# Output products bank by bank with resident weight tiles, and row norms by token tile: a two-block network on one Trainium2 core

## What is computed

```python
def rmsnorm(x, w):
    xf = x.astype(jnp.float32)
    y = xf * lax.rsqrt(jnp.mean(xf * xf, axis=-1, keepdims=True) + EPS)
    return (y * w.astype(jnp.float32)).astype(x.dtype)
...
        xn = rmsnorm(h, mix_norm_w[l])
        proj = xn @ w_in[l]
...
        merged = jax.nn.sigmoid(gate_a) * y_a + jax.nn.sigmoid(gate_b) * y_b
        h = h + merged @ w_mix_out[l]
        h = h + peer_ffn(rmsnorm(h, ffn_norm_w[l]), peer_w_query[l], peer_keys_1[l],
                         peer_keys_2[l], peer_down[l], peer_up[l])
    return rmsnorm(h, final_norm_w)
...
    merged = g_ssd * y_ssd + g_sb * y_sb
    out = jnp.einsum('bld,de->ble', merged, w_out)
    return x + rmsnorm_2(out, norm_post)
```

## Time and profile before

| | us |
|---|---|
| median of three runs | 3337.38 |
| lowest and highest | 3335.16, 3338.36 |
| the profiled execution | 3326.07 |
| its span, first to last instruction | 3324.4 |
| TensorE matmul busy in it | 3052.6 |
| VectorE, ScalarE, POOL busy | 1907.9, 1157.4, 482.5 |

### The profile page before, as it was taken

The page is one execution under the profiler, slowest core; times in us unless marked ns, Lnnn a source line. Parts: engine busy times, 40 slices in busy tenths (PEclk is TensorE's granted clock), DMA queues, the critical chain, the costliest instruction groups (busy, mean ns, idle before and its releaser), DMA issues. The chain is left out here.

```text
span 3324.4 us, 43992 instructions
## 1 busy us (share of the span) xinstructions
PE 3052.6 (92%) x14376; PEld 2458.6 (74%) x14376; DVE 1907.9 (57%) x3582; ACT 1157.4 (35%) x1735; POOL 482.5 (15%) x672
## 2 busy tenths in 40 slices
PE   6999999969897869999999999999996999989996
PEld 4688877757676657788888888888884767866885
DVE  4574444338888968655555565555554674445332
ACT  4443342222236752223323222222233332355222
POOL 1023350000247950000000000000000031024000
PEclk9999999979899989999999999999998989989998
DMA  2220003322223444343333343343332211200331
GB/s 100 76 64 21 26 23 114 103 68 70 70 76 123 180 179 141 123 126 121 118 112 116 126 126 120 120 125 115 126 101 77 86 41 57 89 13 6 122 96 63
DMA packets 136432, 312.39 MB, mean 94 GB/s; under 512 B 9104, under 2 KB 74768, under 8 KB 134160
## 3 DMA queue, kind: packets, MB, share of 16 engines
q1 hardware_dynamic: 136160, 311.00, 28.5%
q10 hardware_dynamic: 176, 0.11, 0.0%
HBM read 273.33 MB, written 37.75 MB: 94 GB/s over the span
## 5 line engine op out<-in xcount | busy, mean ns | idle before, releaser
L180 ACT ACTIVATE split<-raw 128x1024 fp32r<-128x1024 f32 x440 | 455.1, 1054 | 1227.0 <-PE up L1303 457.9
L189 DVE TENSOR_TENSOR split<-raw,split 128x1024 fp32r<-128x1024 f32 x408 | 491.7, 1224 | 551.8 <-ACT split L180 542.1
L1301 PE MATMUL up<-split,weight_high 128*128 128x512 f32 x1024 | 400.4, 391 | 19.6 <-DVE weight_low L1855 19.6
L1302 PE MATMUL up<-split,weight_high 128*128 128x512 f32 x1024 | 399.2, 390 | 0.0
L1303 PE MATMUL up<-split,weight_low 128*128 128x512 f32 x1024 | 399.0, 390 | 0.0
L2001 DVE TENSOR_TENSOR h<-h,up 128x512 f32<-128x512 f32 x416 | 269.3, 683 | 108.1 <-PE up L1303 108.1
L1937 PE MATMUL down<-xh,split 128*128 128x512 f32 x832 | 323.8, 389 | 1.8 <-ACTq L1958 1.8
L1938 PE MATMUL down<-xl,split 128*128 128x512 f32 x832 | 323.7, 389 | 0.0
L1939 PE MATMUL down<-xh,split 128*128 128x512 f32 x832 | 323.6, 389 | 0.0
L1301 PEld LDWEIGHTS up<-split,weight_high 128*128 128x128 f32 x1024 | 192.6, 188 | 63.7 <-issue 19.8
L2306 POOL TENSOR_TENSOR dec<-dec,upto 128x512 f32<-128x512 f32 x16 | 20.0, 1274 | 1483.0 <-ACT dec L2297 1483.0
(11 more groups left out here) (443 smaller groups left out, 5882.5 us busy)
## 6 DMA issues: line engine op xcount, KB each, us to landing
raw<-in_stream SPq DMA_DIRECT2D x440, 512.0 KB, 3.5
gates<-stage SPq DMA_DIRECT2D x16, 2048.0 KB, 6.5
gate<-gates SPq DMA_DIRECT2D x32, 1024.0 KB, 7.4
h<-in_x SPq DMA_DIRECT2D x2, 2048.0 KB, 7.8
rows<-h SPq DMA_DIRECT2D x1, 2048.0 KB, 6.6
h<-rows SPq DMA_DIRECT2D x1, 2048.0 KB, 7.9
out<-res SPq DMA_DIRECT2D x4, 512.0 KB, 2.8
keys<-in_keys SPq DMA_DIRECT2D x1, 1024.0 KB, 4.9
```

Of the source, the lines that this page charges most:

```text
L180: act.activation(g.high[t % slots], g.raw[:, t % RAW, :], ACT.Copy).then_inc(g.high_split, 1)
L189: dve.tensor_tensor(g.low[t % slots], g.raw[:, t % RAW, :], g.high[t % slots], ALU.subtract).then_inc(g.low_split, 1)
L1301: pe.matmul(bank, xh, hi[:, w], start=start, stop=False, skip_group_check=True)
L1302: pe.matmul(bank, xh, lo[:, w], start=False, stop=False, skip_group_check=True)
```

## The change

**Norms by token tile.** A class `TokenNorm` does the norm for one token tile at a time: square, root, scaling, then transposes of its eight 128 x 128 pieces into two banks, and two column steps, each on four chunks at once (128 x 4 x 128). The weight of the norm is now an operand that is broadcast along the tokens, in a tensor_tensor. `opening` replaces `setup` and the first `normed_columns`: one block, h in four transfers, the columns, `ws` and the heads' constants on ScalarE's queue, the two stream splits inside, `ident` made first on POOL. On VectorE each tile's root and scaling stand ahead of the tile before's column steps; a column step waits until the narrow product has used its buffer, and TensorE transposes a tile only behind the narrow products of the one before (`narrow`: eight fp32 products of 128 columns a tile). The second block's `normed_columns` stays.

**Output products bank by bank.** The loops are swapped: bank 0 goes through all eight tiles, then bank 1, and so on. The six tiles beyond the two slots have their own places in SBUF (`out_tile`). `mix_out_norm` is the first block's stage: three PSUM banks in turn for the products, the add behind each bank, the ffn norm of token tile t while later banks are multiplied, and the keys loaded behind the stream. `mix_out_finish` is the last stage: eight banks, and square, root, product, add and store by token tile (stores by half token tile). The old `mix_out`, `finish` and `setup` go.

The diff, cut to its core (the removed functions are in the listing above; what `TokenNorm`'s methods compute is what `normed_columns` computed):

```diff
+    def turn(self, pe, t):
+        pe.wait_ge(self.scaled, t + 1)
+        banks = len(self.turned_ps)
+        for half in range(2):
+            k = 2 * t + half
+            if k >= banks:
+                pe.wait_ge(self.columned, k - banks + 1)
+            for c in range(TT):
+                at = (TT * half + c) * P
+                last = pe.transpose(self.turned_ps[k % banks][:, c * P:c * P + P], self.rows[:, t % 2, at:at + P],
+                                    self.g.ident[:, :])
+            last.then_inc(self.turned, 1)
...
+    def columns(self, dve, t, weight):
+        g = self.g
...
+                if self.small:
+                    dve.wait_ge(self.small_used, k - 1)
+            w = COLS[weight][0] + TT * half
+            dve.tensor_tensor(self.col[:, k % 2, :, :],
+                              self.turned_ps[k % len(self.turned_ps)][:, :].rearrange("p (c n) -> p c n", n=P),
+                              g.cols[:, w:w + TT].unsqueeze(2).to_broadcast([P, TT, P]),
+                              ALU.mult).then_inc(self.columned, 1)
...
+def opening(g, weight, small):
...
+            @block.sync
+            def _(sp):
+                for t in range(TT):
+                    sp.dma_start(g.h[:, t, :], io["x"][t * P:t * P + P, :]).then_inc(rows_loaded[t], 16)
+                for j in range(RAW):
+                    sp.dma_start(g.raw[:, j, :], io["stream"][place(j)]).then_inc(g.raw_loaded[j], 16)
...
+                act.sem_inc(g.tile_used, 2)
+                for t in range(TT):
+                    act.wait_ge(rows_loaded[t], 16)
+                    norm.square(act, t)
+                    norm.root_scalar(act, t)
+                    if t:
+                        norm.split_columns(act, t - 1)
+                    if t >= 2:
+                        split_high(g, act, 0, t - 2)
...
+                pe.wait_ge(ident_made, 2)
+                for t in range(TT):
+                    norm.turn(pe, t)
+                    norm.narrow(pe, t)
...
+def out_bank(g, pe, slots, q, bank, done):
+    w = slice(q // 2 * P, q // 2 * P + P)
+    for c in range(N_OUT):
+        if q == 0:
+            pe.wait_ge(g.low_split, g.base + c + 1)
+        last = mm_rows(pe, slots.high[c], slots.low[c], bank[:, :], g.mh[:, c, w], g.ml[:, c, w], q % 2, c == 0,
+                       c == N_OUT - 1)
+        if q == 2 * TT - 1 and c < N_OUT - 1:
+            last.then_inc(g.tile_used, 1)
+    last.then_inc(done, 1)
+    if q == 2 * TT - 1:
+        pe.wait_ge(done, 2 * TT)
+        pe.sem_inc(g.tile_used, 1)
+def mix_out_norm(g, weight, keys_page):
...
+            @block.sync
+            def _(sp):
+                stream_load_each(g, sp, N_OUT)
+                sp.dma_start(g.keys[:, :, :], g.io["keys"]).then_inc(keys_loaded, 16)
+                sp.wait_ge(keys_loaded, 16)
+            @block.tensor
+            def _(pe):
                 for q in range(2 * TT):
...
+                    if q >= 3:
+                        pe.wait_ge(added, q - 2)
+                    out_bank(g, pe, slots, q, out[q % 3], done)
+                    if q % 2 and q >= 3:
+                        norm.turn(pe, q // 2 - 1)
+                norm.turn(pe, TT - 1)
...
+                for t in range(TT):
+                    act.wait_ge(added, 2 * t + 2)
+                    norm.square(act, t)
+                    norm.root_scalar(act, t)
+                    if t:
+                        norm.split_columns(act, t - 1)
+                for c in range(2):
+                    split_high(g, act, 0, N_OUT + c)
+                norm.split_columns(act, TT - 1)
...
+                for c in range(2, N_OUT):
+                    out_split_low(g, dve, slots, c)
+                for t in range(TT):
+                    for q in (2 * t, 2 * t + 1):
+                        dve.wait_ge(done, q + 1)
+                        rows = g.h[:, t, q % 2 * 512:q % 2 * 512 + 512]
+                        dve.tensor_tensor(rows, rows, out[q % 3][:, :], ALU.add).then_inc(added, 1)
+                    norm.root_vector(dve, t)
+                    norm.scale(dve, t)
+                    if t:
+                        norm.columns(dve, t - 1, weight)
+                norm.columns(dve, TT - 1, weight)
...
+def mix_out_finish(g):
...
+            @block.sync
+            def _(sp):
+                sp.dma_start(wp[:, :], g.io["norm_post"]).then_inc(loaded, 16)
+                stream_load_each(g, sp, N_OUT)
                 for q in range(2 * TT):
...
+                    rows, w = slice(q // 2 * P, q // 2 * P + P), slice(q % 2 * 512, q % 2 * 512 + 512)
+                    sp.wait_ge(added, q + 1)
+                    sp.dma_start(g.io["out"][rows, w], res[:, q // 2, w]).then_inc(stored, 16)
+                sp.wait_ge(stored, 16 * 2 * TT)
...
+            @block.scalar
+            def _(act):
+                for c in range(2, N_OUT):
+                    out_split_high(g, act, slots, c)
+                for t in range(TT):
+                    for q in (2 * t, 2 * t + 1):
+                        act.wait_ge(done, q + 1)
+                        if q:
+                            act.wait_ge(summed, q)
+                        act.activation(junk[:, :], out[q][:, :], ACT.Square,
+                                       accum_out=ss[:, t, q % 2:q % 2 + 1]).then_inc(summed, 1)
+                    act.wait_ge(root, 8 * t + 3)
...
+                    dve.wait_ge(root, n + 4)
+                    n = refine_root(dve, rs, var, tmp, root, n + 4)
+                    dve.wait_ge(root, n)
+                    for q in (2 * t, 2 * t + 1):
+                        w = slice(q % 2 * 512, q % 2 * 512 + 512)
+                        dve.scalar_tensor_tensor(out=res[:, t, w], in0=out[q][:, :], scalar=rs, in1=wp[:, w],
+                                                 op0=ALU.mult, op1=ALU.mult).then_inc(scaled, 1)
+                    for q in (2 * t, 2 * t + 1):
+                        w = slice(q % 2 * 512, q % 2 * 512 + 512)
+                        dve.wait_ge(scaled, q + 1)
+                        dve.tensor_tensor(res[:, t, w], res[:, t, w], g.h[:, t, w], ALU.add).then_inc(added, 1)
     g.base += N_OUT
...
             def _(sp):
-                sp.dma_start(keys[:, :, :], g.io["keys"]).then_inc(keys_loaded, 16)
                 stream_load(g, sp, N_QUERY)
...
-                pe.wait_ge(keys_loaded, 16)
```

More of the change, by code:

```diff
@@ L220, in setup, with constants @@
+def constants(g):
     g.cols = g.const("cols", [P, N_COLS])
@@ new lines, in mix_out_norm, with _ @@
+def mix_out_norm(g, weight, keys_page):
+    nc, base = g.nc, g.base
+    slots = OutSlots(g, (R + 20, R + 24, R + 28, R + 32, R + 36, R + 40))
+    g.keys = g.at("keys", keys_page, [P, 2 * HEADS, N_KEYS])
+    done, added, keys_loaded = g.sem("out_done"), g.sem("rows_added"), g.sem("keys_loaded")
+    with ExitStack() as stack:
+        out = g.banks(stack, 3, "out")
+        norm = TokenNorm(g, R + 44, stack, 4)
+        with nc.Block() as block:
+            @block.sync
[3 more added lines that the diff above has]
+                sp.wait_ge(keys_loaded, 16)
+            @block.tensor
+            def _(pe):
+                for q in range(2 * TT):
+                    if q >= 3:
[4 more added lines that the diff above has]
+                norm.turn(pe, TT - 1)
+            @block.scalar
+            def _(act):
+                for c in range(2, N_OUT):
[4 more added lines that the diff above has]
+                    norm.root_scalar(act, t)
+                    if t:
+                        norm.split_columns(act, t - 1)
+                for c in range(2):
+                    split_high(g, act, 0, N_OUT + c)
+                norm.split_columns(act, TT - 1)
+            @block.vector
+            def _(dve):
+                for c in range(2, N_OUT):
[5 more added lines that the diff above has]
+                        dve.tensor_tensor(rows, rows, out[q % 3][:, :], ALU.add).then_inc(added, 1)
+                    norm.root_vector(dve, t)
+                    norm.scale(dve, t)
+                    if t:
+                        norm.columns(dve, t - 1, weight)
+                norm.columns(dve, TT - 1, weight)
+                for c in range(2):
+                    split_low(g, dve, 0, N_OUT + c)
+    g.base += N_OUT
@@ L2759, in build @@
         rows1 = g.banks(stack, 1, "rows1")[0]
-        g.run(normed_columns, "mix_norm", small=(io["w_ba"], rows1[0:64, :]))
+        g.run(opening, "mix_norm", (io["w_ba"], rows1[0:64, :]))
         g.run(delta_front, act1, rows1)
```

350 lines of the change are left out of this document (190 added, 160 removed).

## The result

| | before | after |
|---|---|---|
| runs, median us | 3336.27 (3326.76 to 3338.36, 4 runs) | 3295.24 (3294.35 to 3298.86, 4 runs) |
| ratio | | 0.9885 [0.9864, 0.9905] |
| profiled execution, us (span) | 3326.07 (3324.4) | 3295.35 (3293.6) |

The change makes the kernel 1.15% faster.

A forecast was written before the change was run, and what follows sets the result against it. TensorE, busy 92%, bounds the kernel; time can be had only where it stands still. Opening -3.1, middle -16.7, end -9.1 sum to -28.9, say -29, carried over to the median 3337.38: 3308.4 us, range 3298 to 3319.

The forecast's parts named there:

- the sum: Whole kernel: opening -3.1, middle -16.7 and end -9.1 us together give -28.9, say -29, against the profiled execution.
- Opening: Kernel start up to front, the first dense matmul: front at 35.3 instead of 40.35, -5.1; net -3.1 us.
- The clock term of +2.0: Opening: front's first eleven matmuls at the low clock, 0.2 us slower each, +2.2, of which 2.0 counted.
- Middle: First block's output products to first query matmul: bank 0 +3.3, transposes +2.4, clock +1.0, tail -23.4; net -16.7 us.
- End: Last output stage: bank 0 with norm_post +4.5, clock +1.0, tail 8.9 instead of 23.5 (-14.6); net -9.1 us.
- No clock lost through all the products: Denies a rival: output products all stay at 1.2 GHz, 36 us lost twice, +43, 3380; chance 0.02.
- The tails empty: Denies a rival: early tiles' adds and norms pile up behind the last bank, about +9, 3346; chance 0.02.
- The tiles are not late: Denies a rival: landings take twice as long, bank 0 waits some 10 us per stage, -16, 3321; chance 0.07.
- none at the changes between Square, Root and Copy: Denies a rival: table loads at each change, nine at 1.28 us in opening and tails, -17, 3320; chance 0.02.
- Nothing later gives the gain back: Denies a rival: something later, through clock phase or transfers, returns the gain, within 0.2%, 3335; chance 0.02.
- Better than counted: Rival for the whole kernel: no clock losses and earlier landings, -37, 3300; chance 0.09.
- The rule against the change: Bank 0, waiting for four tiles one by one, would fall back to the low clock; sum nearer -24 than -29.

The follow-up runs named there:

- the nine: The changed kernel's nine executions, the result's four and five of its unedited repeat: 3294.35 to 3302.52 us, median 3295.7.
- e2: The changed kernel run again without an edit: median 3298.24 us, ratio 0.9887 to the kernel before.
- e3: The kernel before with only the opening changed: median 3322.92 us, ratio 0.9967 to the kernel before.
- e6: The changed kernel with the keys fetched late, by the peer stage: 3305.42 us, one run.
- e4: The kernel before with only the middle changed (first block's output products, ffn norm and keys): median 3315.99 us, ratio 0.9946 to before.
- e11: The changed kernel with the old opening put back: median 3303.24 us, ratio 0.9905 to the kernel before.
- e8: The changed kernel plus idle transposes before cold starts, opening's low splits in VectorE's idle places, norm_post behind the stream tiles: 3297.23 us, ratio 0.9895 to before.
- e5: The kernel before with only the last stage changed: median 3319.74 us, ratio 0.9960 to the kernel before.
- e9: The changed kernel with banks 0 and 1 filled together, low splits in VectorE's idle places, four idle opening transposes, norm_post behind stream tiles: 3282.66 us, ratio 0.9851 to before.
- e10: e9 plus e8's idle transposes behind both merges and the ffn norm's last transposes: 3281.52 us, ratio 0.9842 to the kernel before.

## Why the prediction was wrong

**The step that failed** is first the size of the sum, "-3.1 - 16.7 - 9.1 = -28.9, say -29", and then the level that it was carried over to. Against the median of many executions the change gives -38.0 (3333.7 to 3295.7), 9.0 more than the sum: the opening gave 1.0 more than its term (and not surely), the middle 2.5, the end 1.9 to 3.2, and the rest, some 3, is in no stage. "I carry the difference over to the median" took 3337.38 as that median, from three runs which "themselves spread over 3.2"; 52 executions spread over 19.5, and their median is 3333.7. That is 3.7 us more. The last 0.5 is the result's median against that of the nine. Together 13.2. The range was built on the spread of 3.2 as well, and so it was too narrow; but from a start of 3333.7 the same sum would still have given 3304.7, 9.5 us above what was measured.

That the profiled executions differ by 30.7 (3326.07 to 3295.35), within 2 us of the sum, is no proof of it. That of before was a short draw, 7.6 below its median; that of after lies 0.4 below its own. The short draw hid what the terms had missed, and leaving the carrying over out would have given the right number by luck.

**The terms** are right in kind and together too small:

- Opening: forecast front at 35.3, measured 33.5 to 34.6, where before it lies at 40.4 to 40.9: about -6.6 instead of -5.1. The first tile landed by 4.80, where 5.4 was taken, and the low stream splits ended at 33.25 instead of about 34.1. The clock term of +2.0 was right in kind (0.63 us from 36.20 on), but its size is not shown: the delta stage took 487.6 on average over after, e2, e3 and e6, and 485.1 over the seven runs with the old opening, +2.5, with a scatter of 7 to 11 in each group. Taken as they stand, net -4.1 instead of -3.1.
- Middle: the last product ends 51.3 us after the first instead of 46.2: +5.1 where the parts summed to +6.7. Bank 0 took 11.4 us; before, the first 24 matmuls ended 8.1 us after the first began, not 7.6 as the prediction computed (its 672.0 for bank 0 was as much too early). So +3.3, as forecast. The eight transposes between banks take 0.8 of the product stream each, not 1.2 (one group starts at 686.67, the next product at 687.46). Of the five profiles that have this stage as the change has it and a cold start (after, e2, e4, e6, e11), only e11 has a second slow stretch in it, so +1.0 came out as 0. The tail gave 24.3 (37.3 to 13.0) instead of 23.4. Sum -19.2 instead of -16.7, inside its ends; the transposes (0.8), the clock (1.0) and the tail (0.9) are the terms that were mis-sized.
- End: +4.7 up to the last product instead of +5.5 (51.4 against 46.7), although bank 0 waited 2.71 us for the fifth tile (1.2 of it norm_post's, as forecast) and 13 matmuls ran slow behind that. In e2, e6 and e11 the last product ended only some 3.4 later than before's. The tail gave 15.7 instead of 14.6: behind the last add, which ends at 3290.69, stand 2.9 us of store and end, where 3.8 were carried over from before. Sum -11.0 in this pair, -11.5 to -12.3 in the others; -9.1 forecast.

That is -34.3 to -35.6 by stages against the 38 between the medians; the last 3 us are in no stage that I can name, and lie inside the scatter. Their cause stays open.

**The rivals.** No clock lost through all the products: the last ones take 0.39 us. The tails empty. The tiles are not late: bank 0 waits 2.3 us in the middle, 2.7 at the end, not 10. One load of the root's table stands in the opening (5.96), one each in the two output stages, under the products, and none at the changes between Square, Root and Copy. Nothing later gives the gain back: from the query on, the stages up to the last are as before within their scatter. "Better than counted" (3300) is the rival that came true in size. Of its two reasons the middle's missing clock loss (1.0) and the earlier landing in the opening (0.6) are seen, and they make 1.6 us of the 9.0.

**The rule against the change.** Waits of bank 0 did bring back the low clock in some executions: behind 2.71 us (after, end), 2.47 (e2, end), 1.38 (e11, middle) and 1.40 (e8, middle) stand 7 to 13 slow matmuls, 1.5 to 2.6 us; in e5's last stage seven came behind a wait of only 0.45 that followed one of 1.93. Other waits just as long did not bring it: 1.81 (e6, end), 1.67 (e11, end), 1.46 (e8, end). The longest of these three, in e6, and the wait that follows it:

```profile
3252.91 0.50 PE L1443 MATMUL out<-out_tile,mh 128*128 128x512 f32 x1 [1.81 <-DVE out_tile L1470]
...
3254.19 0.50 PE L1443 MATMUL out<-out_tile,mh 128*128 128x512 f32 x1 [0.31 <-DVE out_tile L1470]
```

So the length of a wait does not tell by itself whether the clock falls; what does is left open here. The Trainium skill (TensorE: Matmul & The Clock Gate, HAM oscillation — how this bites in real kernels) describes this pattern, operand waits after which the next group of matmuls starts cold. This case's traces show it behind some waits and not behind others, and its price, where it comes, is one short stretch and not a slow stage: the sum did not shrink towards -24. Keeping the engine busy ahead (e8) did not mend it. Giving it twice the work per tile did: in e9 banks 0 and 1 have no wait, and no second slow stretch, in either stage.

## What to carry to other kernels

Before you add a difference to a time, ask how far executions of one program lie apart, and take the start from the median of many: three runs were no level here, and one profile is a draw. For the same reason one pair of profiles that fits a sum does not prove the sum; check it stage by stage, over several executions. Two edits that each gain little (order 0.6, token norm 1.8) can gain 12 more together where one produces early what the other can use early. Where work per arriving tile is shorter than the tiles' spacing, take enough accumulators together to cover the spacing, and only then go bank by bank.

## What was not expected of the chip

The granted clock of a fixed program differs from execution to execution (0.961 to 0.968) and the time goes with it by 0.6%, about half of what the change gains. And a start at the high level is no promise: in the opening, in e8 and in e10 TensorE began at 0.47 us per matmul and went down to 0.63 within 1.6 us, without an idle place in between. Nor does a wait decide it: behind 1.38 us the clock fell (e11), behind 1.81 it did not (e6).
